# The load of the keys' and values' weights moved ahead of the second block's parameter loads in the SyncE queue

## The reference, cut to what matters

```python
h = rmsnorm_2(x, norm_mix_pre[l])
proj = h @ w_in[l]                      # 1024 x 3328
q, k, v, u, g_attn, g_ssm = jnp.split(proj, SPLITS, axis=-1)
y_attn = sliding_window_attention(q, k, v, sinks[l], rel_bias) @ w_attn_branch[l]
z = jax.nn.gelu(s5_ssm(u, lam_re[l], lam_im[l], log_dt[l], b_re[l], b_im[l],
                       c_re[l], c_im[l], d_skip[l]))
```

## Time and profile before

| | us |
|---|---|
| runs | 2616.22, 2617.66, 2615.41 |
| median | 2616.22 |
| profiled execution, its own time | 2614.94 |
| its span | 2613.1 |

### The profile page before, as it was taken

One profiled execution on the slowest core, in us unless ns is written; L12 is line 12 of the kernel. 1 busy time (PEld: TensorE's weight loads), 2 busy tenths in 40 slices (PEclk: granted clock), 3 DMA queues, 4 the chain that ended last, 5 costly groups with the idle time before them and its releaser, 6 DMA issues.

```text
span 2613.1 us, 29025 instructions
## 1 busy us (share of the span) xinstructions
PE 2421.8 (93%) x11057; PEld 1929.8 (74%) x11057; DVE 1265.9 (48%) x1569; ACT 827.0 (32%) x927; POOL 862.0 (33%) x198
## 2 busy tenths in 40 slices
PE   6998999999999999999999999997499687999996
PEld 5887766788888888876678888886476565888884
DVE  6566443554432447634345444233865755641634
ACT  4232334332222333333423222232245222421320
POOL 3331232344444433222234444442122022344431
PEclk9999999999999999999899999998699898999997
DMA  4422223344444443213234444433222433344440
GB/s 118 97 65 49 49 65 65 81 97 96 96 92 89 105 86 68 62 39 67 57 81 96 97 96 93 89 77 84 58 49 49 81 65 65 67 95 97 96 97 32
DMA packets 193601, 202.90 MB, mean 78 GB/s; under 512 B 14536, under 2 KB 176472, under 8 KB 193496
## 3 DMA queue, kind: packets, MB, share of 16 engines
q1 hardware_dynamic: 193496, 201.45, 36.2%
HBM read 197.21 MB, written 2.11 MB: 76 GB/s over the span
## 4 chain that ended last, share of the span: by engine, by line
issue 56%; PE 23%; POOL 12%; DVE 6%; DVEq 1%; ACT 1%; DMA 0%; POOLq 0%; ACTq 0%; SPq 0%
POOL w_lo L2284 12%; PE psG L364 7%; PE psG L365 7%; PE psG L366 7%; PE psH L1737 1%; DVE g2a L2201 1%; PE psH L1726 1%; DVE xT L2265 0%; DMA raw<-in_w_in_dram 0%; DVEq L2263 0%; ACT w_hi L357 0%; DVE Wt L1582 0%; DVE rms L460 0%; DVE y L2261 0%; DVE q L2075 0%
## 5 line engine op out<-in xcount | busy, mean ns | idle before, releaser
L2284 POOL TENSOR_TENSOR w_lo<-raw,w_hi 128x2048 fp32r<-128x2048 f32 x186 | 860.3, 4626 | 1698.6 <-ACT w_hi L357 1698.6
L364 PE MATMUL psG<-h_hi,w_hi 128*128 128x512 f32 x1640 | 657.2, 401 | 29.4 <-POOL w_lo L2284 15.5
L357 ACT CAST w_hi<-raw 128x2048 fp32r<-128x2048 f32 x186 | 354.8, 1907 | 982.2 <-PE psG L366 921.9
L365 PE MATMUL psG<-h_lo,w_hi 128*128 128x512 f32 x1640 | 645.9, 394 | 0.0
L366 PE MATMUL psG<-h_hi,w_lo 128*128 128x512 f32 x1640 | 645.6, 394 | 0.0
L364 PEld LDWEIGHTS psG<-h_hi,w_hi 128*128 128x128 f32 x1640 | 312.2, 190 | 139.6 <-issue 52.0
L366 PEld LDWEIGHTS psG<-h_hi,w_lo 128*128 128x128 f32 x1640 | 312.3, 190 | 66.7
L365 PEld LDWEIGHTS psG<-h_lo,w_hi 128*128 128x128 f32 x1640 | 312.9, 191 | 64.2 <-issue 1.4
L364 PE MATMUL psG<-hid_hi,w_hi 128*128 128x512 f32 x608 | 240.6, 396 | 0.0
L366 PE MATMUL psG<-hid_hi,w_lo 128*128 128x512 f32 x608 | 240.2, 395 | 0.0
L365 PE MATMUL psG<-hid_lo,w_hi 128*128 128x512 f32 x608 | 240.2, 395 | 0.0
(11 more groups left out here) (423 smaller groups left out, 3025.2 us busy)
## 6 DMA issues: line engine op xcount, KB each, us to landing
raw<-in_w_in_dram SPq DMA_DIRECT2D x122, 512.0 KB, 6.3
raw<-in_w_gate_dram SPq DMA_DIRECT2D x44, 512.0 KB, 6.0
raw<-in_w_up_dram SPq DMA_DIRECT2D x44, 512.0 KB, 6.0
raw<-in_w_down_dram SPq DMA_DIRECT2D x32, 512.0 KB, 6.2
raw<-in_w_ff_in_dram SPq DMA_DIRECT2D x32, 512.0 KB, 6.3
raw<-in_w_ff_out_dram SPq DMA_DIRECT2D x32, 512.0 KB, 6.0
raw<-in_w_o_dram SPq DMA_DIRECT2D x16, 512.0 KB, 5.6
raw<-in_w_down_dram SPq DMA_DIRECT2D x16, 384.0 KB, 4.8
```

The lines of the kernel that those rows point to most:

```text
L357: act.copy(w_hi[:, s, :], raw[:, s, :]).then_inc(hi_done.sem, 1)
L364: pe.matmul(out, a_hi, b_hi, start=first, stop=False)
L365: pe.matmul(out, a_hi, b_lo, start=False, stop=False)
L2284: pool.tensor_tensor(w_lo[:, s, :], raw[:, s, :], w_hi[:, s, :].bitcast(F32), ALU.subtract)\
```

## The change

One line is moved: SyncE issues the two DMAs of KV right behind those of Q1, ahead of the wait for `x_done` and `d_fold` and of the 17 parameter DMAs. Before, they stood behind these. The instructions of the four compute engines are the same, in the same order.

```diff
         for s in range(2):
             w_src(*un(V_Q + s), w2[:, :, C2_Q + UC * s:C2_Q + UC * (s + 1)], sp)
 
+        w_src(*un(V_KV), w2[:, :, C2_K:C2_U], sp)
         sp.wait_ge(x_done.sem, x_done.at(DEPTH, 0))
         sp.wait_ge(d_fold.sem, d_fold.at(DEPTH, 1))
         with nc.allow_non_contiguous_dma(reason="small parameter layouts"):
...
             for q in range(4):
                 sp.dma_start(d_col[32 * q:32 * q + GC, :], dsk[q]).then_inc(ld2.sem, 16)
-        w_src(*un(V_KV), w2[:, :, C2_K:C2_U], sp)
         for s in range(2):
             w_src(*un(V_U + s), w2[:, 4 * s:4 * s + 4, C2_U:C2_GA], sp)
```

## The result

| | before | changed |
|---|---|---|
| median of 7 runs, us | 2616.22 | 2604.85 |
| lowest to highest | 2610.91 to 2619.21 | 2598.38 to 2608.88 |
| profiled execution: span | 2613.1 | 2604.7 |

The ratio of the runs is 0.995, with an interval of 0.9939 to 0.9961: by it the change makes the kernel about 13 us faster (10 to 16). The two medians lie 11.4 us apart. The forecast was 2603.3, in a range of 2600 to 2609.

The account below looks back on a forecast made before the run. The prediction took the kernel as bound here by a chain of waits from KV's late load to G0. The profiled span, 2614.94 - 12.9 = 2602.0, lay 1.28 us under the median, giving 2603.3; range 2600 to 2609.

Parts of the forecast that it names:

- KV's load at 1752.35, parameters untouched at 1765.04: SyncE's queue: KV issued when GpSimd finishes Q0, 23.2 us earlier; parameters keep their times, with 12.6 us of cover.
- KV's split and the folds share 1765 to 1774, either order is free: GpSimd's split and VectorE's folds overlap; one is held up, both are done by 1774, at no cost.
- KV on TensorE without a gap, end near 1793.7: TensorE starts KV at about 1777.5 at full clock, takes 16.1 us; this leg alone is 15 us earlier.
- U0 lands where KV did, 1783.2: U0's load, issued at KV's old place, lands at 1783.2, so ScalarE splits it 4.54 us earlier.
- The early bound, 1781.4: U0's load landing as fast as a load alone: 1776.2 + 5.2 = 1781.4, with forecast time 2602.1.
- the shift of 14.1: Gain in us at the scaling of q if U0 lands early and U1's split waits for KV's end on TensorE.
- the two cases that I held apart: U0's load landing where KV's did (2603.3) or as fast as alone (2602.1); together given chance 0.76.
- The hold: GpSimd's work on U1 holds VectorE's L1466 until 1802.3; scaling of q ends at 1804.7, 12.9 us earlier.
- G0's split at 1820.7: ScalarE's split of G0 follows the scaling of q at fixed distance, moving from 1833.57, 12.9 us earlier.
- I see nothing that gives the gain back: Rest of the kernel: GpSimd's splits release later loads, so the 12.9 us stays; the rival of later loss had chance 0.07.

Follow-up runs that it names:

- Experiment 3: Loads of KV and U0 both moved ahead of SyncE's wait, against the kernel before: 2600.95 us, ratio 0.9943; fold to store 41.67 us.
- experiment 1: KV's load put behind the wait but ahead of the parameters, against the kernel before: 2609.27 us, ratio 0.9972; fold to store 47.21 us.
- experiment 2: Only U0's load moved ahead of the wait, KV left behind the parameters, against the kernel before: 2618.95 us, ratio 1.001; fold to store 57.28 us.
- Experiment 4: Changed kernel with ScalarE's copies of k and v ahead of its split of U1: 2606.11 us, ratio to the kernel before 0.9963; fold to store 44.88 us.
- experiment 8: Against the kernel before: KV and U0 loads ahead of the wait, ScalarE's copies before U1's split, k scaled before q: 2600.49 us, ratio 0.9941.
- experiment 9: Against the kernel before: KV and U0 loads ahead, copies before U1's split, k before q, last w_attn_branch split after four copies: 2595.23 us, ratio 0.9919.

## Why the prediction was right

- *KV's load at 1752.35, parameters untouched at 1765.04*: 1752.49 and 1765.14.
- *KV's split and the folds share 1765 to 1774, either order is free*: GpSimd got in first, the folds took 8.09 us instead of 3.83 and ended by 1773.8, and TensorE's sums still follow Q1 without a gap.
- *KV on TensorE without a gap, end near 1793.7*: U0's first product starts at 1793.72, at granted clock 1.00.
- *U0 lands where KV did, 1783.2*: its split starts at 1783.23. This was the widest term. Experiment 3 shows that it was the one that set the time, and experiments 1 and 2 that such a landing hangs on how fast the small DMAs ahead of it are issued. The early bound, 1781.4, was misread: I added 5.2 us, the landing of the first half of a unit, to the issue of the second half. A half issued second lands after 6.7 us, which gives 1782.9. So a load alone could not have brought the shift of 14.1, and the two cases that I held apart are nearly one. The forecast did not use this bound.
- *The hold*: L1466 3.56 us where I had put some 3.6, and the shift at the end of the scaling 12.9, measured 12.95 at the store. Experiment 4 is the test of it: the data come earlier, and the store comes later by the 1.2 us that the hold gives.
- *G0's split at 1820.7*: 1820.43.
- *"I see nothing that gives the gain back"*: this was wrong for the profiled execution. L2164 was held 4.1 us, and its span is 2604.7, not 2600.2. I had followed the chain's distances, but not asked how close GpSimd's releases lie to VectorE's operations further on; in the trace of before they were 0.14 us apart. From the last fold to the end 8.5 us were gained in the profiles, not 12.9. The medians moved by 11.4 us. They would agree with the profiles if the kernel before is held in a part of its executions too, which is not shown.

The number came out at 2604.85 against 2603.3, inside the range. At the bias rows' store it is right by its mechanism, term by term. That the median of the whole came within 1.6 us is in part luck: with the tie unseen the sum was 4.4 us too good for the profiled pair, and the runs of either kernel are spread over 8 to 11 us.

## What to carry to other kernels

Ask of a load that is late what stands ahead of it in its queue, and then which wait takes over once it is early: here 15 us were free on TensorE, and 13 were had, since U0's load and GpSimd's hold came next. Look for places where two engines that hold each other up start within a microsecond of each other; here such a tie cost 4.1 us where it fell the wrong way, which hides the effect of other edits, and may be cheaper to remove than the edit that one is studying. Measure a small change from one event ahead of it to one behind it in the same trace, not by whole spans.

## What the runs showed of the hardware

- SyncE issued the 17 small parameter DMAs in 10.5 us with no weight load in flight (kernels before and changed), and in 12.7 and 12.0 us when a load of 1 MB had been issued within 2 us ahead of them (experiments 1 and 2). The pair of 64 KB loads in rows of 64 bytes called `b_im` went from 2.70 us to 4.62 and 4.13; `b_re`, issued just ahead of it with the same shape, took 1.32 us each time.
- A load of 1 MB in two DMAs was used 7.4 us after its issue with nothing issued behind it (experiment 2), and 7.6 us after it with another 1 MB issued right behind it (kernel before).
- Where GpSimd was first, a VectorE operation with two SBUF operands ended 0.54 us (L1466) to 1.1 us (L2164) after GpSimd's. Where VectorE was first, GpSimd's operation was stretched instead: 5.47 us, begun 0.14 us behind, against 4.6. The Trainium skill (SBUF — State Buffer, Who interferes with whom) gives that rule, whoever starts first keeps the other out, and the traces agree. It also says that a copy can take the shared ports, under conditions on its operands. In experiments 8 and 9 the first copy of three elements for each partition was held for 3.04 us until GpSimd ended, and the sixteen copies of one element ahead of it, at 0.13 us each, were not.
